# Weight products that read their moving tile and write their bank from the last column to the first, with weight slots at other addresses

## What is computed

```python
z = h @ w_in                     # mixers, attention, convolution: into a wide z
y_lat = o @ w_out                # and back to 1024
def sq_relu_mlp(h, w1, w2):
    return jnp.square(jax.nn.relu(h @ w1)) @ w2
...
x = layer_norm(DEEPNORM_ALPHA * x + g1 * y, ln_g[l, 0], ln_b[l, 0])
h = modulate(x, sh2, sc2)
x = layer_norm(DEEPNORM_ALPHA * x + g2 * sq_relu_mlp(h, mlp_w1[l], mlp_w2[l]), ln_g[l, 1], ln_b[l, 1])
```

## Time and profile before

| | |
|---|---|
| median of 3 runs | 2625.01 us (2623.85 to 2629.2) |
| span of the profiled execution | 2627.9 us |
| TensorE matmul busy | 2557.7 us, 97% |
| TensorE weight load busy (beside the matmuls) | 2102.4 us, 80% |
| VectorE busy | 1581.3 us, 60% |
| ScalarE busy | 1048.3 us, 40% |
| GpSimd busy | 258.4 us, 10% |
| mean granted clock of TensorE | 0.990 |
| HBM read | 273.92 MB, 105 GB/s over the span |
| instructions | 37789, of them 13070 matmuls |

### The profile page before, as it was taken

One profiled execution on the slowest core, in us unless ns is written; L12 is line 12 of the kernel. 1 busy time (PEld: TensorE's weight loads), 2 busy tenths in 40 slices (PEclk: granted clock), 3 DMA queues, 4 the chain that ended last, 5 costly groups with the idle time before them and its releaser, 6 DMA issues.

```text
span 2627.9 us, 37789 instructions
## 1 busy us (share of the span) xinstructions
PE 2557.7 (97%) x13070; PEld 2102.4 (80%) x13070; DVE 1581.3 (60%) x2460; ACT 1048.3 (40%) x1663; POOL 258.4 (10%) x187
## 2 busy tenths in 40 slices
PE   8999999999999999999989999999999999999997
PEld 6887788888877778888878776788888888888886
DVE  6764665656578866565665786655555665644445
ACT  5334522223347852222353266553223522522333
POOL 2320100000320010000030100310000301300002
PEclk9999999999999999999999999999999999999999
DMA  3221344444320034444432100234444243332222
GB/s 133 73 88 65 118 137 144 144 145 151 135 73 25 26 113 144 144 144 144 144 121 73 41 1 1 81 112 144 144 149 140 96 144 116 104 100 96 96 96 80
DMA packets 79337, 277.46 MB, mean 106 GB/s; under 512 B 8448, under 2 KB 11904, under 8 KB 78720
## 3 DMA queue, kind: packets, MB, share of 16 engines
q1 hardware_dynamic: 58560, 205.55, 23.6%
q10 hardware_dynamic: 20672, 70.51, 8.1%
HBM read 273.92 MB, written 2.10 MB: 105 GB/s over the span
## 4 chain that ended last, share of the span: by engine, by line
PE 85%; DVE 8%; ACT 3%; issue 2%; DMA 1%; POOL 1%; ACTq 0%; DVEq 0%; SPq 0%; POOLq 0%
PE banks L2425 64%; PE banks L2566 5%; PE banks L3002 2%; PE banks L2469 2%; DVE w_lo L1403 1%; PE banks L2944 1%; PE banks L2600 1%; PE banks L2876 1%; DMA w_raw<-weights 1%; PE banks L2853 1%; PE banks L2956 1%; ACT w_hi L679 1%; PE banks L2973 1%; DVE nsa_e L1968 1%; PE banks L2838 1%
## 5 line engine op out<-in xcount | busy, mean ns | idle before, releaser
L679 ACT ACTIVATE w_hi<-w_raw 128x1024 fp32r<-128x1024 f32 x367 | 386.4, 1053 | 621.5 <-PE banks L2425 514.9
L2425 PE MATMUL banks<-h_hi,w_hi 128*128 128x512 f32 x1600 | 628.2, 393 | 1.1 <-DVE w_lo L1403 0.7
L2425 PE MATMUL banks<-h_hi,w_lo 128*128 128x512 f32 x1600 | 623.4, 390 | 0.0
L2425 PE MATMUL banks<-h_lo,w_hi 128*128 128x512 f32 x1600 | 623.2, 389 | 0.0
L1403 DVE TENSOR_TENSOR w_lo<-w_raw,w_hi 128x1024 fp32r<-128x1024 f32 x367 | 474.2, 1292 | 108.7 <-ACT w_hi L679 92.1
L2425 PE MATMUL banks<-g_hi,w_hi 128*128 128x512 f32 (+1 forms) x1108 | 427.7, 386 | 9.8 <-DVE w_lo L1403 8.8
L2425 PE MATMUL banks<-g_lo,w_hi 128*128 128x512 f32 (+1 forms) x1108 | 423.9, 383 | 0.0
L2425 PE MATMUL banks<-g_hi,w_lo 128*128 128x512 f32 (+1 forms) x1108 | 423.7, 382 | 0.0
L2425 PEld LDWEIGHTS banks<-h_hi,w_hi 128*128 128x128 f32 x1600 | 300.5, 188 | 66.5 <-issue 2.8
L2425 PEld LDWEIGHTS banks<-h_lo,w_hi 128*128 128x128 f32 x1600 | 300.6, 188 | 62.8 <-issue 1.7
L2425 PEld LDWEIGHTS banks<-h_hi,w_lo 128*128 128x128 f32 x1600 | 300.4, 188 | 62.9
(11 more groups left out here) (411 smaller groups left out, 3290.8 us busy)
## 6 DMA issues: line engine op xcount, KB each, us to landing
w_raw<-weights SPq DMA_DIRECT2D x384, 512.0 KB, 3.3
ada_raw<-ada ACTq DMA_DIRECT2D x112, 512.0 KB, 3.3
nsa_bias<-nsa_bias ACTq DMA_DIRECT2D x6, 512.0 KB, 3.4
x<-x SPq DMA_DIRECT2D x4, 512.0 KB, 6.6
out<-x SPq DMA_DIRECT2D x8, 256.0 KB, 2.1
mix_cum<-ret_tab ACTq DMA_DIRECT2D x1, 1024.0 KB, 4.7
rows_c<-c_rows ACTq DMA_DIRECT2D x1, 1024.0 KB, 5.6
nsa_w<-cmp_w ACTq DMA_DIRECT2D x1, 1024.0 KB, 5.4
```

The lines of the kernel that those rows point to most:

```text
L679: act.activation(w_hi[s][:], w_raw[s][:], ACT.Copy).then_inc(w_hi_done, 1)
L2425: mm = pe.matmul(bank, w[s][:, k, :], m[:, k, :], start=(n == 0 and a == 0), stop=(n == kts - 1 and a == 2))
```

## The change

It does three things, and the program's order, its waits and its transfers stay as they are.

1. Each weight product reads its moving tile with the columns reversed (`m[:, k, ::-1]`), and writes its bank with the columns reversed (`bank[:, ::-1]`). The weights are read as before, and the bank ends up with the same contents. This is done at L2425 (`unit`), L2469 (`half_steps`), L2566 (`mix_unit`) and L2687 (the first pair of `out0`). The other matmuls, `gate_rows` at L2714 among them, are left as they are.
2. Slot 1 moves from 128 to 192 modulo 512, that is from 0 to 64 bytes from the moving tile; slot 0 stays. Both parts of a slot now lie next to each other. Behind the slots the cursor is brought back to 128 modulo 512, and all that follows lies 512 bytes further on.
3. Slot 3 moves from 448 to 384 modulo 512 (256 bytes from the moving tile) and slot 2 from 448 to 256 (128 bytes from it).

```diff
-        w_hi = [sb(f"w_hi{s}", [P, KT, P], F32R) for s in range(2)]
-        w_lo = [sb(f"w_lo{s}", [P, KT, P], F32R) for s in range(2)]
+        w_hi, w_lo = [], []
+        for s, start in enumerate((128, 192)):
+            cursor[0] += (start - cursor[0]) % 512
+            w_hi.append(sb(f"w_hi{s}", [P, KT, P], F32R))
+            w_lo.append(sb(f"w_lo{s}", [P, KT, P], F32R))
+        cursor[0] += (H_AT - cursor[0]) % 512
...
-        W4, _ = place("more_", ROW_SCALE_AT - 4 * 4 * D, [(f"w_{part}{s}", [P, KT, P], F32R) for s in (2, 3)
-                                                          for part in ("hi", "lo")])
-        w_hi += [W4["w_hi2"], W4["w_hi3"]]
-        w_lo += [W4["w_lo2"], W4["w_lo3"]]
+        more_at = ROW_SCALE_AT
+        for s, start in ((3, 384), (2, 256)):
+            more_at -= 2 * 4 * D
+            more_at -= (more_at - start) % 512
+            made, _ = place("more_", more_at, [(f"w_{part}{s}", [P, KT, P], F32R) for part in ("hi", "lo")])
+            w_hi.insert(2, made[f"w_hi{s}"])
+            w_lo.insert(2, made[f"w_lo{s}"])
...
-                            mm = pe.matmul(bank, w[s][:, k, :], m[:, k, :], start=(n == 0 and a == 0),
+                            mm = pe.matmul(bank[:, ::-1], w[s][:, k, :], m[:, k, ::-1], start=(n == 0 and a == 0),
                                            stop=(n == kts - 1 and a == 2))
...
-                        mm = pe.matmul(bank[:, cols], w[slot][:, k, :], m[:, k, cols], start=(k == 0 and a == 0),
+                        mm = pe.matmul(bank[:, cols][:, ::-1], w[slot][:, k, :], m[:, k, cols][:, ::-1], start=(k == 0 and a == 0),
                                        stop=(k == kts - 1 and a == 2))
```

More of the change, by code:

```diff
@@ L2565, in mix_unit @@
                     for a, (w, m) in enumerate(((w_hi, h_hi), (w_hi, h_lo), (w_lo, h_hi))):
-                        mm = pe.matmul(bank, w[s][:, k, :], m[:, k, :], start=(k == 0 and a == 0),
+                        mm = pe.matmul(bank[:, ::-1], w[s][:, k, :], m[:, k, ::-1], start=(k == 0 and a == 0),
                                        stop=(k == KT - 1 and a == 2))
@@ L2686, in _ @@
                 for a, (w, m) in enumerate(((w_hi, g_hi), (w_hi, g_lo), (w_lo, g_hi))):
-                    mm = pe.matmul(psum[s], w[s][:, k, :], m[:, k, :], start=(k == 0 and a == 0),
+                    mm = pe.matmul(psum[s][:, ::-1], w[s][:, k, :], m[:, k, ::-1], start=(k == 0 and a == 0),
                                    stop=(k == KT - 1 and a == 2))
```

## The result

| | before | after |
|---|---|---|
| median (runs) | 2627.11 us (4, 2623.85 to 2633.36) | 2675.44 us (4, 2674.45 to 2676.81) |
| span of the profiled execution | 2627.9 us | 2673.8 us |
| mean granted clock in it | 0.990 | 0.992 |

The changed kernel is slower: ratio 1.018, 95% interval 1.0164 to 1.0196, 48.3 us. The forecast was 2563 us with slower at 0.29. The range of 2517 to 2700 held the time, but the sign was wrong.

What follows compares the result with a forecast made beforehand. TensorE's matmul pace was taken to bound the kernel. From the 2627.9 us span, 62 us for the reversal and 2.9 us for span against median came off, slots and PSUM writes at 0: 2563 us, range 2517 to 2700.

Steps and rivals of the forecast that it cites:

- What bounds the kernel: Five longest stretches of the chain, 1353.67 us: TensorE's matmul pace alone sets the time; other engines have room.
- the share of 0.89: Part of the affected products' time that stands on the chain: 1876 of 2102 us.
- What the 13 ns are: Full-clock 512-column matmuls: 13 ns beyond their columns, taken as the moving read meeting the next weights' read.
- rival C: All products: collisions on average stay as many whatever the directions, so nothing changes; 2625 us, chance 0.14.
- Three meetings into one: Reversed 512-column products: three meetings of 4 ns per weight load become one, pace 219 ns, 7.5 ns less.
- PSUM written backwards at 0: Reversed bank writes: no cost expected, with an upper bound of 201 ns more for each of 8700 matmuls.
- Rival D: Reversed matmuls: a backward step costs a cycle per column; 4374 us, chance 0.05.
- Slots at 0 +/- 3 ns on half the products: Moved weight slots: new distances from the moving tile priced at no net change, 13 us either way.
- Strong B: L2425 and L2566: weights read first to last, reversal makes three meetings, 248 ns; about 2820 us, chance 0.07.
- milder B: Slot 0: streams starting at one address pay 22 instead of 11 ns, other half gains; 2640 us, milder forms 0.17.
- A: Reversed products: streams in one direction keep clear, meetings vanish, pace 215.5 ns; gain 96, 2529 us, chance 0.24.
- The cover: Low-part writes to the slots: even 170 ns more each stays hidden behind 5.3 us units; 33 us if not.

Runs made afterwards that it cites:

- p4: Probe without the computation: moving tile and weights each kept to a 64-byte quarter of every 256 bytes; 272.7 ns in the same quarter, 243.3 in another.
- e2: The changed kernel with columns read and written forward, its new slots kept; 2655.39 us, ratio 1.0111 to before.
- p3: Probe without the computation: chunk orders, distances stepped up and down, column counts, bf16; at distance 16 it took 226.9 or 233.3 ns.
- e7: The kernel before with reads and writes in chunks of 64 columns, last chunk first, each forward inside; 2629.81 us, ratio 1.0.
- p5: Probe without the computation: weight loads of 16 or 1 column at several places, and other read orders; 1 column took 231.3 or 226.7 ns.
- p1: Probe without the computation: distances in 64-byte steps, read and write directions, column counts; forward 226.6 ns at 0, 233.4 at 64.
- e4: The changed kernel with columns forward, slots 0 and 1 at 256 bytes from the moving tile, 2 and 3 at 320; 2629.33 us, ratio 0.9997.
- e6: The kernel before with only the bank writes reversed, moving tiles read forward; 2629.25 us, ratio 1.0001.
- e3: The changed kernel with its reversed columns kept and the slots put back as before; 2676.33 us, ratio 1.0187.
- p6: Probe without the computation: moving tile read in interleaved 16-byte pieces at eight distances, bank written straight or likewise; 223.3 ns at 176 and 208.
- e9: The kernel before with reads and writes in interleaved 16-byte pieces, weights of all slots at distance 176; 2608.55 us, ratio 0.9913.
- e10: The kernel before with reads and writes in interleaved 16-byte pieces, weights of all slots at distance 208; 2601.67 us, ratio 0.9903.

## Why the prediction was wrong

- **What bounds the kernel: right.** The time followed the pace of TensorE alone. A pace 6.67 ns up, times the counts and the share of 0.89 that the prediction used, gives 51.6 us; 48.3 came.
- **What the 13 ns are: half right.** They do depend on the weights' address. They vanish at half the column rate (426 ns at the half clock), and with half the bytes in each column 2.5 are left (215.8 in bf16). p4 shows by itself that the two reads disturb each other: 273 against 243 ns with nothing changed but the quarter of the weights' addresses. In the Trainium skill, TensorE: Matmul & The Clock Gate, section Part 2, the two reads have independent ports; that gives rival C, no change. e2 (25.4 us from the slots' addresses alone) and p4 contradict it for `fp32r`; the bf16 lines of p3, 215.8 ns at every distance, agree with it.
- **"Three meetings into one": this step failed.** It priced the extra by how far the distance sweeps while the load runs. Three runs show otherwise in its place. The sweep backwards in chunks of 256 bytes costs and gains nothing (e7). A load of 1 column, with no sweep to speak of, has 231 ns at seven places and 226.7 at one, and nowhere 216 (p5). And the period is 256 bytes (p1, e4), not the 512 that I read out of equal k steps; these only require that 512 is a multiple of it. What counts is the order inside 256 bytes: turned round, the read takes 233.3 ns at nearly every distance, 6.7 more than before, where 7.5 less was forecast. The 5 ns less for the half products came out as 1.3 less in slot 0 and 1.8 more in slot 2.
- **The rows under that step were too thin.** It rested on slot 2's 2 ns, read from half products of 256 columns. p1 shows that the sign doesn't carry over: at distance 64 the 256-column product gains 2.2 ns, and the 512-column product loses 6.7. No row of before had 512 columns at any distance but 0. One reading was wrong without changing a number: a plain float32 matmul leaves two records in these traces (L2485 is reached eight times and has 16), so the earlier trace rows is one matmul and the earlier trace rows eight, and the 215 and 107 ns are those of one record.
- **PSUM written backwards at 0: right** (e6, 1.0001). Rival D, two cycles per column, is out. It has beside it the rule of the Trainium skill, PSUM — Partial Sum Buffer, Specifications (TRN2), that non-contiguous patterns slow matmuls significantly; neither the reversed write (227.2 ns) nor the one in 16-byte pieces (227.3) shows that.
- **Slots at 0 +/- 3 ns on half the products: mis-sized and, by itself, wrong in sign.** Forward, distance 64 costs 6.7 ns (e2: 25.4 us). Here it did no harm only because the reversal had already taken it (e3).
- **The rivals.** None names what happened. Strong B (248 ns) needs an extra that grows with the sweep. Its 2820 us, like the prices of milder B and D, were added up without the share of 0.89 that the forecast used. Milder B had the right sign, and its 2640 is nearest in kind, but it put a loss on slot 0 and a gain on slot 1, where both lose the same. A (215.5) was reached by no order that reads the whole row: the lowest paces were 222.7 to 223.3 ns (p5, p6), and one pair of columns read 256 times over had 218.7 (p3).
- **The cover held:** the low part is still 1291 ns on average in its group, as before, and the wait for it fell.

What stays open: what the two modes are in the machine, and of what the 10 ns beyond the 213 ns of columns consist that remain in the quickest of them. The paces that long stretches of the kernels kept, 223.3, 226.7 and 233.3, lie 3.3 ns or a multiple of it apart, 8 columns at 2.4 GHz; what that step is was not shown. Why the order inside 256 bytes matters stays open as well. Nor was it shown why stepping in from distance 32 or from 0 leads to different modes.

## What to carry to other kernels

When TensorE's back-to-back `fp32r` products set the time, the pace of one product is a quantity to measure by itself: with a row read in plain order, put the weights a multiple of 256 bytes from the moving tile, and count on up to 3% more at another distance or with a reversed read. A few nanoseconds that repeat thousands of times need a row of the same shape as the product that pays them; a row at half its columns had the wrong sign. Where a pace has two steady modes, a single profile may catch either, so compare the long stretches one by one before a median is believed.

## What was not expected of the hardware

- The same matmuls at the same addresses run steadily at 226.9 or 233.3 ns, by what ran before them (p3); in e9 a stretch of 1386 products stayed at 233.5 ns and the next at 223.5.
- The pace repeats with 256 bytes of distance: 226.6, 233.4, 232.5, 229.1 and 227.2 ns at 0, 64, 128, 192 and 256.
- Shortening the weight load from 128 columns to 1 never made the product quicker: 231 ns at seven of eight places and 226.7 at the eighth, against 226.7 (p5).
- Reading the moving row in interleaved pieces of 16 bytes makes it faster, 223.3 ns, and with the weights at distance 208 the kernel gains 1.0% (e10).
- The patterns written to PSUM cost nothing, backwards (e6, 1.0001) or in pieces of 16 bytes (p6, 227.3 ns).
- Reading two of every four columns in turn (pieces of 8 bytes, the bank written straight) took 453 ns a product, four of every eight (pieces of 16 bytes) 233 (p4). The Trainium skill, SBUF — State Buffer, section Door 1: The DMA port swizzle, gives lines of 16 bytes and says that two hits on a line in a row are enough for full bandwidth. The 16 bytes agree with these runs (p3 has 226.7 ns, nothing lost, with the order turned round inside them); that two hits are enough doesn't, since pieces of 8 bytes are two hits.
